# Seven block products instead of eight in part of three feed-forwards, and feed-forwards in three parts instead of two

## What is computed

```python
def conv_glu_ffn(h, w_up, conv_w, conv_b, w_down):        # second block, layers 1 and 2
    a, b = jnp.split(h @ w_up, 2, axis=-1)
    a_pad = jnp.pad(a, ((0, 0), (CONV_WIDTH_2 - 1, 0), (0, 0)))
    a = sum(conv_w[j] * a_pad[:, j:j + S] for j in range(CONV_WIDTH_2)) + conv_b
    return (jax.nn.silu(a) * b) @ w_down
# first block: x = x + g2 * ((silu(gt) * up) @ w_ffn_down), gt and up from h @ w_ffn_up
```

## Time and profile before

| | |
|---|---|
| median of 3 runs | 2094.66 us (2092.9 to 2097.76) |
| the profiled execution | 2093.53 us, of which the span is 2091.7 us |
| mean granted TensorE clock | 0.998 |
| PE busy | 2059.9 us, 98% of the span |
| DVE, ACT, POOL busy | 989.1, 885.9, 840.6 us |

### The profile page before, as it was taken

One profiled execution on the slowest core, in us unless ns is written; L12 is line 12 of the kernel. 1 busy time (PEld: TensorE's weight loads), 2 busy tenths in 40 slices (PEclk: granted clock), 3 DMA queues, 4 the chain that ended last, 5 costly groups with the idle time before them and its releaser, 6 DMA issues.

```text
span 2091.7 us, 28578 instructions
## 1 busy us (share of the span) xinstructions
PE 2059.9 (98%) x10618; PEld 1735.8 (83%) x10618; DVE 989.1 (47%) x1909; ACT 885.9 (42%) x1307; POOL 840.6 (40%) x273
## 2 busy tenths in 40 slices
PE   9999999999999999999999999999999999999998
PEld 6888977888888888876877888888887588888887
DVE  4889788574311111376985344034323934431432
ACT  3355545463443222534366453233423954432332
POOL 3443422444244444433713443444443044444443
PEclk9999999999999999999999999999999999999999
DMA  9654322325232432432202433333422034324322
GB/s 371 243 185 125 102 62 66 101 85 178 81 100 81 114 107 78 113 93 65 79 24 64 113 100 93 107 105 94 143 86 73 2 96 121 100 80 121 100 70 91
DMA packets 304008, 220.17 MB, mean 105 GB/s; under 512 B 13520, under 2 KB 288080, under 8 KB 301616
## 3 DMA queue, kind: packets, MB, share of 16 engines
q1 hardware_dynamic: 293216, 195.67, 31.1%
q10 hardware_dynamic: 10704, 23.33, 3.7%
HBM read 213.48 MB, written 2.10 MB: 103 GB/s over the span
## 4 chain that ended last, share of the span: by engine, by line
PE 85%; DVE 7%; issue 3%; ACT 2%; POOL 2%; DMA 0%; ACTq 0%; DVEq 0%; SPq 0%; POOLq 0%
PE bank L912 72%; PE bank L1159 2%; PE bank L1375 2%; PE bank L1353 2%; DVE arena L2811 1%; PE bank L1307 1%; DVE small L2809 1%; PE bank L1362 1%; PE bank L1458 1%; PE bank L1207 1%; POOL w_split_out L2851 1%; DVE bank L2277 1%; POOL w_split L2851 1%; PE bank L1218 1%; PE bank L1540 1%
## 5 line engine op out<-in xcount | busy, mean ns | idle before, releaser
L912 PE MATMUL bank<-h_hi,w_split 128*128 128x512 f32 x3696 | 1119.4, 382 | 1.8 <-DVE arena L2679 1.1
L2851 POOL TENSOR_TENSOR w_split<-wslots,w_split 128x2048 fp32r<-128x2048 f32 (+3 forms) x174 | 712.7, 4097 | 987.9 <-ACT w_split L1613 549.5
L912 PEld LDWEIGHTS bank<-h_hi,w_split 128*128 128x128 f32 x3696 | 698.7, 189 | 116.8 <-issue 15.7
L912 PE MATMUL bank<-h_lo,w_split 128*128 128x512 f32 x1848 | 701.8, 380 | 0.0
L912 PEld LDWEIGHTS bank<-h_lo,w_split 128*128 128x128 f32 x1848 | 349.7, 189 | 51.2 <-issue 3.4
L912 PE MATMUL bank<-hid_hi,w_split 128*128 128x512 f32 x1056 | 316.2, 380 | 2.2 <-DVEq L2562 2.2
L1634 ACT ACTIVATE w_split<-wslots 128x2048 fp32r<-128x2048 f32 (+2 forms) x80 | 141.4, 1767 | 368.0 <-PE bank L912 368.0
L1613 ACT ACTIVATE w_split<-wslots 128x2048 fp32r<-128x2048 f32 (+3 forms) x91 | 158.8, 1745 | 300.8 <-PE bank L912 278.9
L912 PEld LDWEIGHTS bank<-hid_hi,w_split 128*128 128x128 f32 x1056 | 199.6, 189 | 32.3 <-issue 3.6
L912 PE MATMUL bank<-hid_lo,w_split 128*128 128x512 f32 x528 | 200.1, 379 | 0.0
L2277 DVE SCALAR_TENSOR_TENSOR bank<-arena,cols,bank 128x512 f32<-128x512 f32 x240 | 161.3, 750 | 5.4 <-ACT bank L1727 4.9
(11 more groups left out here) (341 smaller groups left out, 2352.4 us busy)
## 6 DMA issues: line engine op xcount, KB each, us to landing
wslots<-in_f_w_up SPq DMA_DIRECT2D x88, 512.0 KB, 4.7
wslots<-in_w_in SPq DMA_DIRECT2D x24, 1024.0 KB, 5.3
wslots<-in_w_ffn_up SPq DMA_DIRECT2D x44, 512.0 KB, 4.5
arena<-in_w_ada ACTq DMA_DIRECT2D x8, 2048.0 KB, 9.1
wslots<-in_f_w_down SPq DMA_DIRECT2D x16, 768.0 KB, 4.8
wslots<-in_a_w_in SPq DMA_DIRECT2D x10, 1024.0 KB, 5.2
wslots<-in_f_w_down SPq DMA_DIRECT2D x16, 640.0 KB, 4.4
arena<-in_w_ada_first SPq DMA_DIRECT2D x8, 1024.0 KB, 19.3
```

What stands on the lines that cost most here:

```text
L912: return nc.tensor.matmul(bank[:], w, woven(x), start=start, stop=stop)
L2851: last = nc.gpsimd.tensor_tensor(part[:, 1, cols_of], slot(p, 1, size)[:, 0, cols_of], part[:, 0, cols_of].bitcast(F32), ALU.subtract)
```

## The change

PARTS replaces HALVES: every feed-forward is done in three parts of 8, 8 and 6 hidden tiles, so there are nine down stages instead of six, with kc = 8, 8 and 6 instead of 12 and 10; the number of down matmuls is the same. Every part now begins its down stage with `first_downs`, in a new order.

In each part every second up job (even index 2i; in the first part only from the third pair of jobs on) becomes a unit of `seven_products`: 2 + 4 + 3 = 9 of 22 jobs for each feed-forward, 27 in all. The job is seen as a 2 x 2 block product (gate and up columns by the two halves of the contraction, and the two halves of the tokens), and seven products of sums of blocks take the place of eight: each has 4 tiles of contraction, 3 matmuls each and 256 token columns, which makes 84 matmuls of 128 x 256.

What feeds them: the sums of the activations over blocks, made once for each feed-forward (`whole_tokens` on POOL for feed-forward 0, eight ACT copies for 1 and 2, four DVE subtractions of 1024 elements in `token_sums_made` ahead of the first turn, `token_upper`, `token_lower`); for each unit four DVE sums of weight blocks (`three_sums`, `fourth_sum`, 512 elements, both inputs in SBUF), seven ACT upper parts and seven POOL lower parts of 512 elements (`entry_lowers`); and after the products one small ACT copy and six DVE sums over banks (`early_sums`, `late_sums`). The other up job of a pair is an ordinary one; ACT and POOL split its weights in two halves. Loops of the up stages are written out. Constants, columns, semaphores and buffers are moved to make room; that changes no work.

```diff
-HALVES = ((0, 12), (12, FT - 12))
+PARTS = ((0, 8), (8, 8), (16, FT - 16))
+LAST = len(PARTS) - 1
+SEVEN = (0, 1, 2)
...
+def seven_at(k, part, i):
+    return k in SEVEN and (0 if part else 2) <= i < PARTS[part][1] // 2
...
+def down_bank(name, j):
+    return banks[2 * one(name, 0)[0] + 1] if name[:3] == "ffn" and j == 1 else banks[2 * one(name, j)[0]]
...
         def tiles(q, first, end):
             for c in range(first, end):
-                if q == p:
-                    pe.wait_ge(S[waits[0]], waits[1] + c + 1)
+                pe.wait_ge(S[waits[0]], waits[1] + c + 1)
                 for wp, hp in ((0, 0), (0, 1), (1, 0)):
-                    last = product_of(banks[2 * q], w[q][wp][:, c, :], rhs(c, hp), c == 0 and wp + hp == 0, c == kc - 1 and wp == 1)
+                    last = product_of(banks[2 * p + (q != p)], w[q][wp][:, c, :], rhs(c, hp), c == 0 and wp + hp == 0, c == kc - 1 and wp == 1)
             if end == kc:
                 last.then_inc(product_done[q], 1)
...
+        start_split(name, 0)
+        tiles(p, 0, kc - 1)
+        pe.wait_ge(lo_ready[other], SPLITS_BEFORE[FIRST[name] + 1] + 1)
+        tiles(other, 0, kc - 1)
+        tiles(p, kc - 1, kc)
+        tiles(other, kc - 1, kc)
...
+    def seven_products(k, part, i):
...
+        q, use = one(name, 2 * i)
+        pe.wait_ge(bank_free[q], use + 1)
+        for e, bank, at, tokens in ((0, 7, 0, 2), (1, 7, 1, 0), (2, 6, 1, 1), (4, 6, 0, (0, 0)), (3, 2 * q, 1, (1, 1)), (5, 2 * q, 0, (1, 0)), (6, 2 * q + 1, 0, 3)):
+            if e < 6:
+                pe.wait_ge(S["sums_lower"], LOWER[unit] + e + 1)
+            else:
+                pe.wait_ge(lo_ready[q], SPLITS_BEFORE[FIRST[name] + 2 * i] + 1)
+            for c in range(DT // 2):
+                for wp, hp in ((0, 0), (0, 1), (1, 0)):
+                    if isinstance(tokens, int):
+                        x = token_sums[tokens][hp][:, 2 * c:2 * c + 2, :].rearrange("p a b -> p b a")
+                    else:
+                        x = woven(h_split[hp][:, DT // 2 * tokens[0] + c, :])[:, tokens[1] * P:(tokens[1] + 1) * P, :]
+                    last = nc.tensor.matmul(banks[bank][:, at * HALF:(at + 1) * HALF], entries[k][e][wp][:, c, :], x,
+                                            start=c == 0 and wp + hp == 0, stop=c == DT // 2 - 1 and wp == 1)
...
+        last.then_inc(product_done[q], 1)
+    def up_part(k, part):
+        name = f"ffn{k}_up{part}"
+        for i in range(JOBS[name] // 2):
+            if i == part == 0:
...
+                split_job(start_split(name, 0), DT, 2 * P, h_parts, waits, late=f"ffn{k}" if k else None)
+            elif seven_at(k, part, i):
+                seven_products(k, part, i)
+            else:
+                split_job(start_split(name, 2 * i), DT, 2 * P, h_parts, None)
+            split_job(start_split(name, 2 * i + 1), DT, 2 * P, h_parts, None)
...
     def ffn(k):
...
+        for part, (t0, n) in enumerate(PARTS):
+            up_part(k, part)
+            first_downs(f"ffn{k}_down{part}", n, lambda c, half: hid[half][:, c, :], ("hid_ready", 2 + FT * k + t0))
...
+    def sum_uppers(k, part, i):
+        for e, made in enumerate((1, 3, 4, 4)):
+            act.wait_ge(S["angle_then_sum_ready"], SUMS[k, part, i] + made)
+            nc.scalar.activation(entries[k][e][0][:], entry_sums[k][e], ACT.Copy).then_inc(S["softplus_then_sums_upper"], 1)
+    def block_uppers(k, part, i):
+        n = FIRST[f"ffn{k}_up{part}"] + 2 * i
+        act.wait_ge(weights_in[n % 2], LOADED[n])
+        act.wait_ge(product_done[n % 2], slot_before(n) // 2 + 1)
+        for e, block in ((4, (0, 0)), (5, (0, 1)), (6, (1, 1))):
+            nc.scalar.activation(entries[k][e][0][:], block_of(k, *block), ACT.Copy).then_inc(S["softplus_then_sums_upper"] if e < 6 else hi_ready[n % 2], 1)
...
+                    last.then_inc(S["softplus_then_sums_upper"], 1)
+        for part, (t0, tiles) in enumerate(PARTS):
...
+            for i in range(tiles // 2):
+                following = (k, part, i + 1) if seven_at(k, part, i + 1) else None
+                p, use = one(name, 2 * i)
+                if i == 0 and seven_at(k, part, 0):
+                    first_product(k, part, 0)
+                if following:
+                    sum_uppers(*following)
+                    block_uppers(*following)
+                else:
+                    split_job(slot_after(FIRST[name] + 2 * i))
+                conv_or_gate(2 * i, p, use)
+                gate_and_upper(2 * i, p)
+                if i == part == 0 and k in SEVEN:
+                    token_upper(k, 2)
+                    token_upper(k, 0)
+                p, use = one(name, 2 * i + 1)
...
+                if i + 1 < tiles // 2:
...
+                    first, second = slice(0, SLOT // 2), slice(SLOT // 2, SLOT)
...
+                    nc.scalar.activation(w_split[p][:, 0, first], raw[:, first], ACT.Copy).then_inc(S["softplus_then_sums_upper"], 1)
+                    conv_or_gate(2 * i + 1, p, use)
+                    nc.scalar.activation(w_split[p][:, 0, second], raw[:, second], ACT.Copy).then_inc(hi_ready[p], 1)
+                else:
+                    split_job(ahead)
+                    conv_or_gate(2 * i + 1, p, use)
+                gate_and_upper(2 * i + 1, p, following)
+                if i == part == 0 and k in SEVEN:
+                    token_upper(k, 1)
+                    token_upper(k, 3)
+            if part < LAST:
+                for j in range(DT):
+                    n = slot_after(FIRST[down] + j)
+                    if seven_at(k, part + 1, 0) and n == FIRST[f"ffn{k}_up{part + 1}"]:
+                        sum_uppers(k, part + 1, 0)
+                        block_uppers(k, part + 1, 0)
+                    else:
+                        split_job(n)
...
+    def token_sums_made(k):
...
+        dve.wait_ge(*ready(0))
+        sum_of(0, 2, 0)
+        dve.wait_ge(*ready(1))
...
+        sum_of(2, 1, 2)
...
+        sum_of(1, 1, 0)
...
+        sum_of(3, 3, 1)
+    def sum_of_blocks(k, e, a, b, op):
+        nc.vector.tensor_tensor(entry_sums[k][e], a, b, op).then_inc(S["angle_then_sum_ready"], 1)
+    def three_sums(k, part, i):
+        n = FIRST[f"ffn{k}_up{part}"] + 2 * i
+        dve.wait_ge(weights_in[n % 2], LOADED[n])
...
+        sum_of_blocks(k, 0, block_of(k, 0, 0), block_of(k, 1, 0), ALU.subtract)
+        sum_of_blocks(k, 1, block_of(k, 1, 0), block_of(k, 1, 1), ALU.add)
+        dve.wait_ge(S["angle_then_sum_ready"], SUMS[k, part, i] + 2)
+        sum_of_blocks(k, 2, entry_sums[k][1], block_of(k, 0, 0), ALU.subtract)
+    def fourth_sum(k, part, i):
+        dve.wait_ge(S["angle_then_sum_ready"], SUMS[k, part, i] + 3)
+        sum_of_blocks(k, 3, block_of(k, 0, 1), entry_sums[k][2], ALU.subtract)
...
+    def early_sums(k, part, i):
...
+        dve.wait_ge(S["softplus_then_sums_upper"], UPPER[k, part, i, "first"])
+        steps.did(nc.vector.tensor_tensor(first[:, HIGH], banks[6][:, HIGH], first[:, LOW], ALU.add))
+        steps.settle()
...
+        steps.did(nc.vector.tensor_tensor(halves(sums), both, halves(banks[7][:]), ALU.add))
+    def late_sums(k, part, i):
+        q, use = one(f"ffn{k}_up{part}", 2 * i)
...
+        dve.wait_ge(product_done[q], use + 1)
+        steps.settle()
+        steps.did(nc.vector.tensor_tensor(gates[:, LOW], gates[:, LOW], first[:, LOW], ALU.add))
...
+        last = nc.vector.tensor_tensor(ups[:, HIGH], banks[7][:, HIGH], sums[:, LOW], ALU.add)
...
+    def up_part(k, part, turn):
+        name, tiles = f"ffn{k}_up{part}", PARTS[part][1]
+        for i in range(tiles // 2):
+            following = (k, part, i + 1) if seven_at(k, part, i + 1) else None
+            unit = seven_at(k, part, i)
+            if unit and i == 0:
+                early_sums(k, part, 0)
+            if following:
+                three_sums(*following)
+                if unit:
+                    dve.wait_ge(S["g_turned_then_products"], PRODUCTS[k, part, i] + 2)
+                else:
+                    q, use = one(name, 2 * i)
+                    dve.wait_ge(product_done[q], use + 1)
+                fourth_sum(*following)
+            if unit:
+                late_sums(k, part, i)
+            turn(2 * i, None)
+            turn(2 * i + 1, (lambda: early_sums(*following)) if following else None)
...
+            if seven_at(k, part + 1, 0):
+                if j == DT - 3:
+                    three_sums(k, part + 1, 0)
+                if j == DT - 2:
+                    fourth_sum(k, part + 1, 0)
...
+    def entry_lowers(k, part, i):
+        n = FIRST[f"ffn{k}_up{part}"] + 2 * i
+        for e, block in enumerate((None, None, None, None, (0, 0), (0, 1), (1, 1))):
+            hi, lo = entries[k][e]
+            if e < 6:
+                pool.wait_ge(S["softplus_then_sums_upper"], UPPER[k, part, i, e])
+            else:
+                pool.wait_ge(hi_ready[n % 2], SPLITS_BEFORE[n] + 1)
```

(37 more changed lines are left out.)

302 lines of the change are left out of this document (217 added, 85 removed).

## The result

The changed kernel takes 2173.92 us (median of 4 runs, 2170.07 to 2177.03) against 2095.97 us before: 1.0373 times as long, 95% interval 1.0348 to 1.0397. The forecast was 2155, in a range of 2096 to 2180. So the direction and the range held, and the sum came out 19 us too low.

A forecast was written before the change was run, and what follows sets the result against it. PE, busy for 98% of the span, was taken to bound the kernel, so every new wait adds. Terms -26.5 + 28.2 - 1.4 + 5.8 + 27.6 + 20.8 + 7.2 = +61.7 us on 2093.53 gave 2155, range 2096 to 2180.

The forecast's parts named there:

- products, 27 units of 9.38 us: Up stages: 84 matmuls of 128 x 256 take 9.38 us instead of 10.36 for each unit, -26.5 us.
- starts of nine down stages: First down jobs: PE idles 3.4 us (kc = 8) or 2.6 us (kc = 6) for the third job's weights, +28.2 us.
- waits of before gone, last hidden tile: Down stages: old waits of 2.6 us go, the last hidden tile comes 0.6 us late twice, -1.4 us.
- starts of the feed-forwards: Before third up jobs: token sums on DVE delay the turn, 8.0 us each, plus 1.8 us later twice, +27.6 us.
- starts of parts two and three: First unit's lower parts delay the ordinary job 1.6 us six times, next unit 2.8 us four times, +20.8 us.
- between units in feed-forwards 1 and 2: Steady units: DVE needs 20.6 us against PE's 19.74, 0.9 us eight times, +7.2 us.
- last down stages with kc = 6: Tiles 4.55 us apart exceed shorter down jobs of 3.88 us: 4.6 us in feed-forward 0, 1.2 in 1, +5.8 us.
- granted clock: Whole kernel: clock is 0.998 although PE already pauses for 2%, so new pauses lose nothing by it, 0 us.
- (a): Rival: DVE and POOL block each other more rarely at feed-forward starts, part starts and steady units; 33.8 less, 2121 us; chance 0.22.
- (b): Rival: only PE's own order and the last stage cost, DVE and POOL work is hidden; +6, 2100 us; chance 0.12.
- (c): Rival: PE is never kept waiting, 26.5 + 2.6 us saved, 2064 us; chance 0.08.
- (d): Rival: DVE loses to POOL on every weight sum, two more pieces of 1.27 us in twelve units; +30, 2185 us; chance 0.08.

The follow-up runs named there:

- fill_less: Changed kernel plus 7 (with six hidden tiles 5) plain float32 matmuls with discarded results between the first two down jobs and the third; 2159.49 us.
- two_halves: Changed kernel with down jobs of one parity taking turns between the two halves of their split copy; 2132.67 us.
- combo_root: two_halves plus earlier token sums in feed-forward 0, parts of 6, 8, 8 tiles, and token copies and sums ahead of root and reciprocal; 2108.45 us.
- pool_waits: Changed kernel with POOL holding back the third up job's lower part in feed-forwards 1 and 2 until DVE's four token sums are made; 2168.36 us.
- first_only: Against the kernel before: units and three parts only in feed-forward 0; feed-forwards 1 and 2 in halves without units, first down jobs reordered; 2085.59 us.
- best: combo_root with some weight sums in feed-forwards 1 and 2 after the turn, and first jobs of two last down stages finished earlier; 2108.64 us.
- parts_only: Changed kernel with three parts and the new down starts but no units, all 66 up jobs ordinary; 2158.64 us.

## Why the prediction was right, and where its sum was off

The direction came from one reading, that PE was at 98% with no idle time to hide a new wait in, and it held. By its own steps (spans: +61.7 forecast, +82.9 measured):

| step | forecast | measured |
|---|---|---|
| products, 27 units of 9.38 us | -26.5 | -26.5 (from the pace, 0.1117 us again) |
| starts of nine down stages | +28.2 | +27.1 |
| waits of before gone, last hidden tile | -1.4 | -2.6 |
| starts of the feed-forwards | +27.6 | +25.5 |
| starts of parts two and three | +20.8 | +13.5 |
| between units in feed-forwards 1 and 2 | +7.2 | 0 |
| last down stages with kc = 6 | +5.8 | +9.4 |
| pauses longer than listed | 0 | +4 |
| granted clock | 0 | +30 |

The measured terms of the waits are sums of PE's gaps on the timeline. With the other terms they add up to +80; the rest, some 3 us, is not placed.

**The step that failed** is the sentence "I count no loss of it from the new pauses". Its argument was that PE already paused for 2% at a clock of 0.998. But what those pauses leave at 2.4 GHz says nothing of longer ones: the new gaps are of 2 to 7 us, and the trace of after has 1.2 GHz for 3.4 or 6.8 us at most of them, eighteen such stretches where before had two (one of them, in each, at the very end of the kernel). One row each of fill_less and two_halves shows that the clock stays at 1.00 where the gap is closed. The cost, 30 us, is as large as all the waits at the down starts.

**Down starts.** The term stood on durations for 1280 elements scaled to 1024 and 768, and each of the six gaps at kc = 8 was 3.06 us, forecast 3.4. At kc = 6 the gaps were 3.57, 2.91 and 2.26, forecast 2.6; the first two are not POOL's but DVE's (`DVEq L686`), late with the first bank of the last stage. So that term came out right as a sum while two of its nine gaps had another cause than the one it was built on. The hidden tile, forecast to be 0.6 us late twice, was never what PE waited for, +1.2 in the forecast.

**Starts of the feed-forwards.** Third jobs waited 7.14, 6.76 and 6.78 us, forecast 8.0 each; the units after them 2.62 and 2.18, forecast 1.8.

**Parts two and three, and steady units.** The ordinary job waited 0.15 to 0.44 us, forecast 1.6 (1.8 us in all against 9.6), the next unit 2.2 to 3.1 in feed-forwards 1 and 2, forecast 2.8, and 0.8 in feed-forward 0, forecast 0. Between steady units PE never waited. DVE's weight sums by form (count, then total busy us and mean ns):

```profile
L2799 DVE TENSOR_TENSOR entry_sum<-wslots 128x512 f32<-128x512 f32 x54 | 45.8, 889 | 52.7 <-DMA wslots<-in_f_w_up 32.1 <-DMA wslots<-in_w_ffn_up 17.6 <-DVE hid_lo L2773 2.8
L2799 DVE TENSOR_TENSOR entry_sum<-wslots,entry_sum 128x512 f32<-128x512 f32 x27 | 39.3, 1457 | 4.2 <-PE bank L1020 2.1
L2799 DVE TENSOR_TENSOR entry_sum<-entry_sum,wslots 128x512 f32<-128x512 f32 x27 | 24.8, 920 | 0.9
```

So the blocking is there, about one blocked sum for a unit, as assumed: the fourth takes 1.46 us in the mean instead of 0.69. What was too high is the rest of the layout. A window over one steady unit and the job behind it, and DVE's only idle time for PE in it:

```profile
1382.39:1402.13 19.74, 19.74 (x133) 18.39 (x133) 14.32 (x22) 10.04 (x16) 14.34 (x9) 1.00 0.39 107
...
1382.59 0.70 DVE L3087 TENSOR_TENSOR bank<-bank,rstd 128x512 f32<-128x512 f32 x1 [0.43 <-PE bank L1020]
```

PE is busy for all of its 19.74 us, and DVE waits 0.43 us for it. DVE's chain takes 19.3 us, not the 20.6 that were laid out. "DVE is at the edge" was right, on the other side of it: the 20.6 was too much by 1.3 us. The sum of some twenty durations can't decide a question of 0.9 us, and the term should have stood in the range, not in the sum.

**Last stages.** Tiles of feed-forward 0 were 4.62 us apart, forecast 4.55, and lost 0.47 to 0.74 each:

```profile
879.73 0.48 PE L1020 MATMUL bank<-hid_hi,w_split 128*128 128x512 f32 x1 [3.57 <-DVEq L686]
890.19 0.48 PE L1020 MATMUL bank<-hid_hi,w_split 128*128 128x512 f32 x1 [0.74 <-DVEq L686]
...
910.38 0.48 PE L1020 MATMUL bank<-h_hi,w_split 128*128 128x512 f32 x1 [2.18 <-POOL w_split L3177]
```

That is 2.2 us. Two waits behind the short stages were not foreseen: 2.18 us for the first weights of the next layer, and 5.11 us at the memory product after feed-forward 1. With eight tiles in the last stage (combo_root) the second is gone and the first is 1.5. Which transfer was behind the second was not tried.

**The rivals.** (a), 2121, needed DVE and POOL to miss each other, and (b), 2100, needed their work to be hidden; pool_waits shows that they meet, and the 39 us of waits at the starts of feed-forwards and parts show that the work isn't hidden. (a) was right in part: starts of parts and steady units, 28 us in the forecast, measured 13.5. (c), PE never kept waiting, is not this kernel, but first_only is what it looks like when it comes true for nine units. (d), 2185, lies nearer to the measured time than the forecast does, but for the wrong reason: a unit had about one blocked sum, not three.

## What to carry to other kernels

On an engine that is never idle, count each new pause twice, as the wait and as what the clock behind it may cost: here 73 us of waits lost 30 us more by the clock, and the loss differs from run to run. Before an eighth of the products is bought with work on three other engines, look at how long the slowest of them needs for one turn: the units paid where a turn on DVE took 2.9 us and gave nothing where it took 7. (The turn was not changed by itself, so that it is the turn is argued, not shown.) And when a wait is moved rather than removed, expect it one job later; a buffer that was half empty was worth 41 us, the last re-ordering of DVE's work (best) nothing.

## What the runs showed that was not expected

- Gaps of 3.06 us brought TensorE down to 1.2 GHz for the next 3.4 us in which it was busy, six times of six in the changed kernel and three of six in parts_only. Work whose results are thrown away kept it at 2.4 GHz: granted clock 1.00 instead of 0.91 over 20 us.
- Twelve plain float32 matmuls of 128 x 256 took 5.0 us, 0.42 us each, where the fast float32 mode takes 0.1117 for the same shape, and each leaves two records in the trace.
- POOL suffers from the meeting with DVE as well, if less: its subtraction of 2048 elements took 5.06 us instead of 4.57 while DVE's sum stood until it was done.
